# Weight remainders on VectorE, gate products among the projection units, a float32 bias product: a hybrid decoder layer

## What is computed

```
xn = rms_norm(x);  z = xn @ w_in                    # 7 parts of 1024 columns
rnn_x, rnn_gate, q, k, v, g_rnn, g_attn = split(z)
xc = causal_conv4(rnn_x);  hr = rg_lru(xc)          # two block-diagonal gates, then h = a*h + u over time
y_rnn  = (hr * gelu(rnn_gate)) @ w_proj_rnn
y_attn = attention(rotary(q), rotary(k), v) @ w_proj_attn      # 8 heads of 128, 32 of them rotated
x  = x + (sigmoid(g_rnn)*y_rnn + sigmoid(g_attn)*y_attn) @ w_out
hn = rms_norm(x)
x  = x + moe(hn)        # top 4 of 32 experts: clamped SwiGLU of hn @ w_gu + b_gu, then @ w_down + b_down
out = rms_norm_final(x)
```

## Time and profile before

| | |
|---|---|
| median of 3 runs | 1229.68 us (1229.4 to 1229.72) |
| the profiled execution | 1229.34 us |
| its span, mean granted TensorE clock | 1227.6 us, 0.972 of full speed |
| busy: PE, PEld | 1133.2 us (92%), 589.9 us (48%) |
| busy: DVE, ACT, POOL | 340.2, 219.6, 221.3 us |
| DMA | 450.16 MB, mean 367 GB/s |
| stage one ends (last product of unit 39) | 303.56 us |

### The profile page before, as it was taken

How to read it: one execution, slowest core, us unless ns; L and a number is a source line. 1 busy time by engine, 2 the same in 40 slices (tenths; PEclk the granted TensorE clock), 3 DMA queues, 4 the chain that set the end, 5 groups by cost and what they waited for, 6 DMA issues and landing times.

```text
span 1227.6 us, 17186 instructions
## 1 busy us (share of the span) xinstructions
PE 1133.2 (92%) x7358; PEld 589.9 (48%) x7358; DVE 340.2 (28%) x589; ACT 219.6 (18%) x361; POOL 221.3 (18%) x99
## 2 busy tenths in 40 slices
PE   8869879999999999988989999989999999989897
PEld 8859879999433333333333333333333333333332
DVE  5982676422511112121111111111111211111112
ACT  5436645644300000000000000000000000000002
POOL 7838866686000000000000000000000000000000
PEclk9979889999999999999999999999999999999999
DMA  9434426659899999999999999999999999999995
GB/s 279 150 137 146 145 88 242 227 211 419 367 417 432 429 428 428 431 432 430 431 432 431 432 431 431 429 430 431 432 430 428 431 430 427 430 429 431 431 428 223
DMA packets 46615, 450.16 MB, mean 367 GB/s; under 512 B 6288, under 2 KB 8400, under 8 KB 29008
## 3 DMA queue, kind: packets, MB, share of 16 engines
q1 hardware_dynamic: 46288, 448.80, 88.0%
q0 software_dynamic: 144, 0.52, 0.1%
q10 hardware_dynamic: 144, 0.26, 0.1%
HBM read 448.00 MB, written 1.05 MB: 366 GB/s over the span
## 4 chain that ended last, share of the span: by engine, by line
DMA 44%; PE 39%; issue 8%; POOL 7%; ACT 1%; DVE 1%; SPq 0%; POOLq 0%; DVEq 0%
DMA dn<-in_w_down 34%; PE ps L710 13%; PE ps L689 12%; DMA gu<-in_w_gu 10%; POOL w_lo L411 6%; PE ps L464 2%; PE ps L461 2%; PE ps L460 2%; PE ps L663 1%; PE ps L630 1%; PE ps L484 1%; PE ps L480 1%; PE ps L479 1%; PE ps L704 0%; PE ps L676 0%
## 5 line engine op out<-in xcount | busy, mean ns | idle before, releaser
L689 PE MATMUL ps<-gu,xg 128*64 128x512 f32 x2048 | 451.1, 598 | 12.9 <-DMA gu<-in_w_gu 12.9
L689 PEld LDWEIGHTS ps<-gu,xg 128*64 128x64 f32 x2048 | 146.8, 138 | 299.4 <-issue 275.0
L710 PE MATMUL ps<-dn,actT 128*64 128x512 f32 x992 | 234.0, 623 | 42.0 <-DMA dn<-in_w_down 41.8
L411 POOL TENSOR_TENSOR w_lo<-land,w_hi 128x1024 fp32r<-128x1024 f32 x80 | 216.2, 2730 | 76.6 <-ACT w_hi L848 76.5
L1334 DVE TENSOR_SCALAR g<-ps 128x512 f32<-128x512 f32 x32 | 22.1, 692 | 670.1 <-PE ps L689 670.1
L710 PEld LDWEIGHTS ps<-dn,actT 128*64 128x64 f32 x992 | 70.4, 142 | 196.2 <-issue 124.4
L460 PE MATMUL ps<-x_hi,w_hi 128*128 128x256 f32 x384 | 96.9, 290 | 5.2 <-ACT w_hi L848 3.1
L461 PE MATMUL ps<-x_lo,w_hi 128*128 128x256 f32 x384 | 95.8, 286 | 0.0
L848 ACT ACTIVATE w_hi<-land 128x1024 fp32r<-128x1024 f32 x80 | 80.1, 1052 | 55.2 <-PE ps L464 39.4
L460 PEld LDWEIGHTS ps<-x_hi,w_hi 128*128 128x128 f32 x384 | 75.0, 195 | 5.7 <-issue 5.5
L461 PEld LDWEIGHTS ps<-x_lo,w_hi 128*128 128x128 f32 x384 | 75.1, 195 | 0.1
(11 more groups left out here) (258 smaller groups left out, 936.9 us busy)
## 6 DMA issues: line engine op xcount, KB each, us to landing
gu<-in_w_gu SPq DMA_DIRECT2D x56, 4096.0 KB, 29.9
dn<-in_w_down SPq DMA_DIRECT2D x62, 2048.0 KB, 23.6
gu<-in_w_gu SPq DMA_DIRECT2D x16, 2048.0 KB, 13.2
land<-in_w_in SPq DMA_DIRECT2D x13, 2048.0 KB, 8.1
land<-in_w_proj_rnn SPq DMA_DIRECT2D x2, 2048.0 KB, 9.1
land<-in_w_proj_attn SPq DMA_DIRECT2D x2, 2048.0 KB, 8.3
land<-in_w_out SPq DMA_DIRECT2D x2, 2048.0 KB, 7.9
land<-in_w_in SPq DMA_DIRECT2D x2, 1024.0 KB, 8.3
```

The source lines that it names most:

```text
L411: pool.tensor_tensor(w_lo[:, q % PIECES], land[q // PIECES][:, :, (q % PIECES) * P:(q % PIECES + 1) * P], w_hi[:, q % PIECES].bitcast(f32) ...
L689: last = mm(ps[64 * h:64 * h + 64, 4 + c, :], xg[:, k * SLOTS:(k + 1) * SLOTS], gu[par][m // 2][:, m % 2 * 2 + r, c * D + h * HALF:c * D + ...
L710: last = mm(ps[64 * h:64 * h + 64, bank, :], src[:, j, half * SLOTS:(half + 1) * SLOTS], dn[half][:, j, h * HALF:(h + 1) * HALF], start=ha ...
```

## The change

- GpSimd's loop over the remainders goes; `split_lo(q)` on VectorE makes them, written by hand among its other work. GpSimd makes its small constants as soon as the gates have been read.
- The gate products stand behind units 5 to 8, two slices behind each; the loops over units are unrolled. ScalarE's sigmoids follow the same units. Tanh, exp, square and square root move to other units.
- The convolutions, the products of the gates' input, the rotation (in halves of four heads) and the scan (in halves of four slices) are placed between remainders. The gated output moves into the attention rounds of heads 1 and 2.
- The swap of the rotated rows is issued from ScalarE's queue.
- b_gu stays float32 in four groups of 32 rows by 512 columns (`b4`), `bsel` and `ident4` are float32, and each of the four bias products uses 32 rows.
- At the start: vecs are loaded from ScalarE's queue, block 0 in pieces of 128, 128 and 256 columns, the square sum of the second half of x is made on VectorE, both scales come from one square root and one reciprocal, and ScalarE scales the second half.

```diff
-            with pool.Fori(0, N_BLK // LAND, 1) as it:
-                for q in range(PIECES * LAND):
...
+            pool.wait_ge(gates_read, KT)
             pool.memset(zrow[:, :], 0.0).then_inc(zrow_ready, 1)
...
+            def split_lo(q):
+                dve.wait_ge(hi_ready, q + 1)
+                p = q % PIECES
+                V.tensor_tensor(w_lo[:, p], land[q // PIECES % LAND][:, :, p * P:(p + 1) * P],
+                                w_hi[:, p].bitcast(f32), ALU.subtract).then_inc(lo_ready, 1)
...
+            for h in range(16):
+                pe.wait_ge(evicted, h + 1)
+                transposed(h, h % 4, x_hi, x_lo, first=h == 0)
+                if 5 <= h < 9:
+                    lru_gates(2 * (h - 5))
+                    lru_gates(2 * (h - 5) + 1)
...
-                    pe.wait_ge(rope_done, 2)
+                    pe.wait_ge(rope_done, 4)
...
-                        mm(ps[64 * h:64 * h + 64, 4 + c, :], bsel[par][:, :],
-                           bias3[:, c * D + h * HALF:c * D + (h + 1) * HALF], start=True, stop=False)
+                        rows = slice(32 * (2 * c + h), 32 * (2 * c + h) + 32)
+                        mm(ps[64 * h:64 * h + 64, 4 + c, :], bsel[par][rows, :], b4[rows, :], start=True, stop=False)
```

ScalarE's order from unit 5 on, after:

```diff
+            for h in range(5):
+                turn(h)
+            A(spare, spare, ACT.Sigmoid)
+            for h in range(5, 9):
+                turn(h)
+                lru_sigmoids(2 * (h - 5))
+                lru_sigmoids(2 * (h - 5) + 1)
...
+            for h in range(11, 13):
                 turn(h)
-                for j in range(4 * (h - 12), 4 * (h - 12) + 4):
+                if h == 11:
+                    swap_rope(0, z_q)
+                for j in range(4 * (h - 11), 4 * (h - 11) + 4):
                     A(sa[:, j, :], sa[:, j, :], ACT.Exp, scale=cneg[:, j:j + 1]).then_inc(a_ready, 1)
-            turn(14)
-            act.wait_ge(sxc_ready, 1)
+            turn(13)
+            act.wait_ge(sxc_ready, 2)
             act.wait_ge(a_ready, KT)
             A(xc[:, :, :], sa[:, :, :], ACT.Square).then_inc(a2_ready, 1)
+            turn(14)
+            act.wait_ge(m2_ready, 1)
+            A(th[:, :, :], th[:, :, :], ACT.Sqrt).then_inc(mult_ready, 1)
             turn(15)
+            swap_rope(1, z_k)
             act.wait_ge(evicted, 4 + 8)
             A(z_gate[:, :, :], z_gate[:, :, :], ACT.Gelu_apprx_tanh).then_inc(gelu_ready, 1)
```

VectorE's order, after:

```diff
+            for h in range(2, 6):
+                split_lo(2 * h)
+                conv(2 * (h - 2))
+                split_lo(2 * h + 1)
+                conv(2 * (h - 2) + 1)
+            split_both(6)
...
+            for h in range(7, 11):
+                split_both(h)
+            gate_input(0)
+            split_both(11)
+            split_both(12)
+            gate_input(1)
+            split_both(13)
+            split_both(14)
             dve.wait_ge(rope_landed, 32)
-            rotate(0, z_q)
+            rotate(0, z_q, 0)
+            split_both(15)
+            rotate(0, z_q, 1)
             dve.wait_ge(a2_ready, 1)
...
+            split_both(16)
+            split_both(17)
+            dve.wait_ge(sxc_ready, 2)
             dve.wait_ge(mult_ready, 1)
             link(V.tensor_tensor(sx[:, :, :], sx[:, :, :], th[:, :, :], ALU.mult))
...
+            split_both(18)
+            rotate(1, z_k, 0)
+            split_both(19)
+            rotate(1, z_k, 1)
+            split_both(20)
+            scan(range(4))
...
             for i in range(H):
                 mask_and_max(i)
+                split_both(21 + i)
+                if i == 1:
+                    gate_output()
                 if i >= 2:
                     keep_o(i - 2)
                 normalise(i)
+                if i == 0:
+                    scan(range(4, KT))
+                if i == 2:
+                    leave_gated()
```

More of the change, by code:

```diff
@@ L127, in program @@
         sel = [at(f"sel{i}", 180 + i / 4, [P, TT, SLOTS], bf16) for i in range(2)]
-        bsel = [at(f"bsel{i}", 180.5 + i / 8, [96, SLOTS], bf16) for i in range(2)]
+        bsel = [at(f"bsel{i}", 180.5 + i / 4, [P, SLOTS]) for i in range(2)]
         dn_last = [at(f"dn_last{h}", 16 * h, [P, DN_RUN, D]) for h in range(2)]
@@ L190, in program @@
         gathered_half, xg_half = sem("gathered_half"), sem("xg_half")
-        first_landed, spare_ready = sem("first_landed"), sem("spare_ready")
+        first_landed, spare_ready = [sem(f"first_landed{i}") for i in range(2)], sem("spare_ready")
         w_landed = [sem(f"w_landed{i}") for i in range(LAND)]
@@ L292, in _ @@
                 if u == 0:
-                    sp.dma_start(land[0][:, :, 0:256], src[:, :, 0:256]).then_inc(first_landed, 16)
+                    for i in range(2):
+                        sp.dma_start(land[0][:, :, P * i:P * i + P], src[:, :, P * i:P * i + P]).then_inc(
+                            first_landed[i], 16)
                     sp.dma_start(land[0][:, :, 256:512], src[:, :, 256:512]).then_inc(w_landed[0], 16)
@@ L297, in _ @@
                 if u == 1:
-                    for q in range(3):
-                        sp.dma_start(b96[32 * q:32 * q + 32, :], b_gu[0]).then_inc(b96_landed, 16)
+                    for q in range(4):
+                        sp.dma_start(b4[32 * q:32 * q + 32, :], b_gu[0, :, q * HALF:(q + 1) * HALF]).then_inc(
+                            b4_landed, 16)
                     sp.wait_ge(bd_zeroed, 1)
@@ L309, in _ @@
                     sp.dma_start(rbb[:, :], router_b[0:1, :].to_broadcast([P, N_E])).then_inc(rbb_landed, 16)
-                for i, (z, after) in enumerate(((z_q, 7), (z_k, 9))):
-                    if u == after:
-                        sp.wait_ge(evicted, 4 + (12, 16)[i])
-                        for half in range(2):
-                            sp.dma_start(rot[i][16 * half:16 * half + 16, :, :],
-                                         z[16 * (1 - half):16 * (1 - half) + 16, :, :]).then_inc(rot_landed[i], 16)
                 if u == 17:
@@ L493, in natural, with lru_gates @@
                 last.then_inc(filled, 1)
-            def z_halves(first):
-                with pe.Fori(0, 2, 1) as it:
-                    for h in range(first, first + 4):
-                        pe.wait_ge(evicted, 4 * it + (h + 1))
-                        transposed(h, h % 4, x_hi, x_lo, base=8 * it, first=h == 0)
-            z_halves(0)
-            pe.wait_ge(wx_landed, 32)
-            pe.wait_ge(wa_landed, 32)
-            for j in range(KT):
+            def lru_gates(j):
+                if j == 0:
+                    pe.wait_ge(wx_landed, 32)
+                    pe.wait_ge(wa_landed, 32)
                 pe.wait_ge(xc_ready, j + 1)
@@ L886, in _, with lru_sigmoids @@
                 act.nop().then_inc(evicted, 1)
-            for h in range(8):
-                if h == 7:
-                    A(spare, spare, ACT.Sigmoid)
-                turn(h)
-            for j in range(KT):
+            def lru_sigmoids(j):
                 act.wait_ge(gates_filled, j + 1)
@@ L1094, in _ @@
                                        op0=ALU.mult, op1=ALU.subtract).then_inc(xT_ready, 1)
+            for q in range(1, PIECES):
+                split_lo(q)
             dve.wait_ge(expap_ready, 1)
@@ new lines, in gate_input, with rotate @@
+            def gate_input(half):
+                dve.wait_ge(gates_read, 4 * half + 4)
+                js = slice(4 * half, 4 * half + 4)
+                V.tensor_tensor(sx[:, js, :], sx[:, js, :], xc[:, js, :], ALU.mult).then_inc(sxc_ready, 1)
+            def rotate(i, z, half):
+                if half == 0:
+                    dve.wait_ge(rot_landed[i], 32)
+                heads = slice(4 * half, 4 * half + 4)
+                z, r = z[0:ROPE, heads, :], rot[i][:, heads, :]
+                cos, sin = (t[:, :].unsqueeze(1).to_broadcast([ROPE, 4, T]) for t in (cos_t, sin_t))
+                V.tensor_tensor(z, z, cos, ALU.mult)
+                link(V.tensor_tensor(r, r, sin, ALU.mult))
+                V.tensor_tensor(z, z, r, ALU.add).then_inc(rope_done, 1)
@@ new lines, in scan @@
+            def scan(js):
+                for j in js:
+                    ins = V.tensor_tensor_scan(out=xc[:, j, :], data0=sa[:, j, :], data1=sx[:, j, :], initial=0.0,
+                                               op0=ALU.mult, op1=ALU.add)
+                link(ins)
+            for h in range(2, 6):
+                split_lo(2 * h)
+                conv(2 * (h - 2))
+                split_lo(2 * h + 1)
+                conv(2 * (h - 2) + 1)
+            split_both(6)
+            V.memset(gates[:, :, :], 0.0)
```

137 lines of the change are left out of this document (65 added, 72 removed).

## The result

| | before | after |
|---|---|---|
| median of the runs | 1229.62 us (1229.4 to 1229.72, 4 runs) | 1199.86 us (1198.72 to 1201.84, 4 runs) |
| ratio of the medians | | 0.976, 95% interval 0.9748 to 0.9772 |
| the profiled execution, its span | 1229.34, 1227.6 us | 1201.84, 1200.1 us |
| last product of stage one | 303.56 us | 272.2 us |
| expert 0's first weight product | 315.43 us | 284.33 us |

The kernel is faster by 2.4%. The forecast of 1204.8 us had the direction and the mechanism, and 4.9 us too little gain. In the profiled execution 31.1 us are won before expert 0 and 3.6 given back behind it.

What follows compares the result with a forecast made beforehand. Bound: the expert weight stream, whose end moves with the start of expert 0's products. From 1229.34 us: unit 22 -28.15, clock +2.9, small waits -0.3, bias +0.7, together -24.85: 1204.5, by the median 1204.8; range 1194 to 1214.

Steps and rivals of the forecast that it cites:

- Bound and lever: Expert stage is one weight stream at 430 GB/s; the end moves with the start of expert 0's products.
- Remainders: 80 subtractions moved to VectorE at 1.14 to 1.2 us each, beside 112 us of its own work.
- Gates: Convolutions done by 46.0, no stall, gate pairs cost 1.72 us a unit; all of 15.4 and 4.6 us returns.
- Rotation: Before unit 19, the scores need all four rotation halves: TensorE waits 4.3 us, 129.1 to 133.4.
- four scans (1.38 each): VectorE's scan groups before normalise(1), due at 158.8; TensorE waits 5.6 us behind unit 21.
- The second term: the clock: Slow TensorE products behind the two new waits: 0.6 us for the first, 2.3 for the second, +2.9 in all.
- Bias: Float32 bias products ahead of expert 0's weight products: +0.7 us, bounds +0.4 and +3.0; hidden in other experts.
- rival 1: VectorE's queue meets both deadlines, no new waits, 38.6 us come back less the bias: 1191.8 us; chance 0.10.
- rival 2: Rounds of units 22 to 27 late by 1.5 us, six of them costing 9: 1213.8 us; chance 0.12.
- rival 3: Shared PSUM banks serialise the bias products, at most +3.0 us for +0.7: 1207.1 us; chance 0.12.
- rival 4: VectorE bounds stage one, remainders at 2.4 us each, some 12 us slower: 1242 us; chance 0.03.
- rival 5: Stage one ends earlier but the weight stream does not start earlier, no gain: 1230 us; chance 0.03.

Runs made afterwards that it cites:

- The second profile: Changed kernel, unchanged, profiled once more: first weight product at 282.82 us, from there 915.4 us to the end of the span.
- the rotation's edit: Both halves of k's rotation put ahead of unit 19's remainders, against the changed kernel: 1194.82 us, ratio 0.9722.
- the doubled bias: The four float32 bias products of every expert issued twice, against the changed kernel: 1198.59 us.
- the gates behind unit 7: All eight gate pairs and ScalarE's sigmoids together behind unit 7, not two behind each of units 5 to 8, against the changed kernel: 1199.51 us.
- the early counts: ScalarE's four free counts given ahead of its splits of pieces 1 to 3, against the changed kernel: 1198.83 us, ratio 0.976.

## Why the prediction was right, and where it was off

**Bound and lever: right.** The end moved with expert 0's first weight product, 31.1 us earlier, and the stream kept its 430 GB/s. "Near 290" was 284.33, and unit 22, expected near 161 to 163, started at 157.83.

**Remainders: right.** 1219 ns for 1218, 80 of them in 94.6 us. What was off is VectorE's own work: 112 us estimated, 82.4 measured, because the relief from GpSimd reached more forms than I had taken. Constants, convolutions and rotations gave back 29 us for the 20 estimated; the scan gave 6.3 and the remainders of mix 3.0, both entered at nothing.

**Gates: right.** No wait in units 2 to 18, and gate pairs at their own price. Unit 9 starts at 72.95 for 71.5, unit 16 at 113.45 for 111.8. The 1.5 us come from the start: unit 0 begins 0.3 us later than before, and its products slow down from 14.2 to 17.6 us (its second piece starts 4.16 us after the first instead of 2.9). The second profile doesn't have this (clock 1.00 over 12 to 24 us for 0.86), so it comes and goes with the execution.

**Rotation: right in its place, shorter than said.** A wait of 4.3 us until 133.4 was predicted; it was 2.95 us until 133.84. The first profile stands 1.5 us late from its start on. In the second TensorE arrives at 129.4 for 129.1 and the rotation is done at 132.4 for 133.4: VectorE's chain was 1.0 us shorter than in the walk. The chain also runs through ScalarE's issues of the q swap, which the walk doesn't name.

**The step that failed in size: "four scans (1.38 each)".** They take 0.60 us each (four in 2.42). The row I took the earlier trace rows was measured beside GpSimd, and I corrected the scalings and convolutions for that but not the scan. normalise(1) was due at 158.8 and done at 156.15, 2.65 us earlier; with TensorE also 2.1 us later, mostly by the slow products behind the first wait, the predicted wait of 5.6 us became 0.95, outside the 4 to 6 that were named as the sign of being right. Unit 22 starts at 157.83 for 160.5: 2.7 us of the error.

**The second term: the clock.** I charged 2.3 us for the slow products behind the second wait and 0.6 for those behind the first. Behind 0.95 us there are none: from unit 22 to the bias it took 125.48 us where 126.32 + 2.9 - 0.3 = 128.9 was forecast, 3.4 us of the error. The first wait's slow products I had called "mostly hidden by VectorE's chain". They are not: the rotation's edit and the doubled bias, without them, go from the scores to the transposes of L520 in 20.8 us, the changed kernel in 22.4. That is 1.6 us, which lie ahead of unit 22. The chain there runs through TensorE itself, over ScalarE's split.

**Bias: right.** 0.46 became 1.02, +0.56 for +0.7.

**Sum.** 2.7 + 3.4 + 0.1 = 6.2 us more gain before expert 0 than predicted, and 3.6 us given back in the expert stage, entered at 0 (2.4 in the wait for the last weights, whose cause is open, and 1.5 by the clock of the last up half): 1201.84 against 1204.5 for the profiled execution. That the two errors partly cancel there is luck. The low end of the bounds was also added up wrong: -0.8, a clock term of 0 and no waits make 1191 and not 1195. The measured median lies within either.

**Rivals.** New waits stayed small, so the outcome lies between the forecast and rival 1 (1191.8). The late rounds of units 22 to 27 (rival 2), the banks in turn (rival 3), a remainder of 2.4 us (rival 4) and an unmoved stream (rival 5) are each ruled out by a row above.

**The parts of the gain**, by the first weight product:

| | us | step |
|---|---|---|
| before | 315.43 | |
| float32 bias alone | 303.21 | -12.2 |
| and the new order, start and swap | 293.29 | -9.9 |
| and remainders on VectorE | 284.33 | -9.0 |
| and the rotation ahead of unit 19's remainders | 280.52 | -3.8 |

By medians of the whole the four steps are -9.1, -8.6, -12.2 and -5.0 us.

Each row is one profile, good to about 1.5 us. The parts aren't independent: the bias frees time in which convolutions run, and remainders on VectorE without the new order were not tried.

## What to carry to other kernels

Before an operation is moved off GpSimd, take the durations of the target engine's other work from rows in which GpSimd is idle, for every form and not only for the ones that look odd. A mean over a group hides this, for it mixes instructions that met the other engine with some that didn't; look at single ones in order of time. A DMA that a computing engine issues takes that engine's time (here 0.6 us each), and counts where its queue is the link that others wait for; the rotation's edit with the swap back on SP's queue was not tried. When engines meet in a loop, a saving counts only where the loop's last link is the engine that saves; walk the queue link by link, and place what TensorE waits for ahead of what it needs a unit later.

## What the runs showed of the hardware

- The price of GpSimd's subtractions (128x1024, both inputs in SBUF) to VectorE, read from instructions in order of time: four scans of 256 elements 8.91 us beside them and 2.42 in a pause; three convolution steps of 253 to 255 columns 5.51 and 1.52 (float32 bias alone); a 128x128 scaling up to 2.13 us, ending with the subtraction that was running, and 0.29 in a pause.
- A wait of 2.95 us in front of the scores was followed by slow products in both profiles of the changed kernel (clock 0.95 over 130 to 165 us), with the gates behind unit 7 and with the early counts, and by none with the doubled bias (clock 1.00). Waits of 1.45 and 0.68 us there were followed by none.
- The granted clock over 400 to 800 us, in the stream, is 0.98 in both profiles of before and 1.00 in all ten with the float32 bias. The time doesn't gain by it, since the stream sets it.
- Four float32 products of 32 rows by 512 columns, two to a PSUM bank, hold the array for 0.85 us together, as one of 128 rows and 512 columns does (0.86).
- With remainders on GpSimd the time spreads over 10 us (1209.42 to 1219.45); no other kernel here spreads over more than 5.3.
